# A fused two-block transformer kernel: first projections on an accumulator's bank, pieces and waits moved, and the compression's first layer on four column groups

## The chip, the cores and the metric

The kernel runs on one core of one Trainium2 chip. The metric is the device time of one execution in microseconds, the median of three runs. The kernel is one program in which TensorE (matmul), VectorE, ScalarE, GpSimd and SyncE (which issues the DMAs) each run their own list of instructions and wait for one another on semaphores.

## The reference

The input is one sequence of 256 tokens with 1024 features. Two layers with adaptive norms come first. Each takes six vectors of scales, shifts and gates from a conditioning vector, `silu(c) @ ada_w + ada_b`. Layer 0 mixes with a state-space part and latent attention, layer 1 with gated linear attention (GLA) and a sparse attention (NSA); each is followed by a SwiGLU network of width 2816. A second block follows with windowed attention and a gated MLP side by side, cross attention over 256 memory rows, and a lookup among 16384 experts (PEER). What the change touches, cut down:

```python
h = rmsnorm(x, pre) * (1.0 + scale) + shift          # ahead of every stage
gq, gk, gv, glr, gg, nq, nkv, ngate = split(h @ w_in)  # layer 1's projections
log_a = log_sigmoid(glr @ w_gk2 + b_gk) / 16
swiglu = (silu(h @ w_gate) * (h @ w_up)) @ w_down

def compress(z, w1, w2):                             # NSA, for keys and for values
    zb = z[:, win_idx] + cmp_pos                     # 15 windows of 32 tokens, 2 groups
    zb = zb.reshape(b, 15, 2, 32 * 64)               # 30 rows of 2048
    return silu(zb @ w1) @ w2                        # w1 is 2048 x 256
```

All products keep fp32 precision.

## The kernel before

**Weights.** A weight matrix comes in slabs of 128 x 2048 fp32 through a ring of three slots (`raw`). Each slab is two blocks of 1024 columns. For a block, ScalarE writes the rounded high part `whi` (`cut_hi`, L2583) and then VectorE or GpSimd the remainder `wlo` (`cut_lo`, L1487; which of the two `lo_engine` says: VectorE for the projections, by turns for the feed-forward slabs, GpSimd for the second block of the slabs in `FIRST` and for most of the peer stage). The ring of `whi`/`wlo` has three blocks, so a block's high part waits until TensorE has used the block three before it (`emptied`). A product takes three matmuls: high x high, high x low of the activations, low x high (`pe_mm3`, L601 to L603). SyncE sends the slabs in one fixed order, each when the slab three before it has been cut.

**Ada pieces.** The conditioning weights come as 0.5 MB pieces (`ADA`), two at a time in `ada_ring`. VectorE multiplies each into an accumulator (`ve_ada`, L1513, L1516). After each fourth piece TensorE sums it over partitions (`pe_ada`, L807, 8 matmul records), and VectorE adds the bias (L1505). Where the calls stand in the two engines' lists decides when the work is done. `pe_ada` also notes before which slab SyncE is to issue the next piece (`W.due() - sooner`), and SyncE then waits until the piece two before it has been used.

**Banks.** PSUM has eight banks. `Banks.take` gives the next one of the current order (`ALL` all eight, `ROT` banks 4 to 7, `ACC` the accumulators 0 to 3) and makes TensorE wait until the bank's last holder was read.

**A norm and the first projection.** At a junction the row norms are made by ScalarE and VectorE, `pe_norm` transposes the eight feature tiles into four banks (L740), with a few matmuls of no use to keep TensorE at work (L734, L723). ScalarE then writes the high part of each tile (`se_normed`, L2712 or L2710), VectorE the low part (`ve_normed`, L1599 or L1582) and only with that the banks are marked as read. The first projection (`pe_first`) goes tile by tile: high parts (L657, and L659 with the first half's low weights) for tiles 0 to 3, then the products with the low parts of h (L663) for 0 to 3, the same for 4 to 7, and last the second half's low weights (L670). This happens ahead of `ffn0` (about 237 us), `mix1` (440), `ffn1` (688), `mix2` (883) and the peer stage (1131).

**mix1.** Slabs w_gqk 0, w_glr 0, w_gqk 1 to 3. After w_gqk 1 TensorE computes `log_a` (L1080), VectorE copies it (L2006), ScalarE takes Abs, Exp, Ln, and VectorE the log gate and a scan (L2011 to L2018).

**mix2.** `ve_mix2` waits for the tables cos2 and sin2, which are sent once `ffn1` has ended, before it cuts the blocks of w_mqk.

**The compression.** `ve_windows` (L2123) gathers the 30 windows into `zb`, 16 tiles of 128 x 30. `pe_cmp_hidden` (L1181) multiplies them with 16 tiles of the raw fp32 slab, 128 x 256 each, and sums into 30 partitions. ScalarE applies Silu (L2990), `pe_cmp_turn` transposes (L1190), VectorE copies (L2130). Kind 0 is the keys, kind 1 the values. Between the two stand the GLA states (L1156 on TensorE, L2084 and L2086 on VectorE), the projection w_nq 1 and several ada pieces; the GLA outputs (L1139, L1142) follow. Then come w_nks and w_nvs and, at 607.71 us, the first use of the compression's results (L1247). An fp32 matmul leaves two records in the trace.

Of the kernel before, what the change touches and what calls it, by code (L numbers as in the profile page):

```python
# [39 lines left out]
      ("inv", 1), ("sgn", 1), ("j16", 16), ("ind", 8), ("pick", 16)]  # L40
# [275 lines left out]
class Memory:  # L316
# [90 lines left out]
    def second_layer(self):  # L407
# [18 lines left out]
        self.w2, self.zb, self.hid = alloc(256, 4, 64), alloc(480, 16, 30), alloc(256)[0:30, :]  # L426
# [125 lines left out]
class Net:  # L552
# [70 lines left out]
    def pe_linear(self, e, name, i, kt, nn, xh, xl, split=None, eager=False, ada=True):  # L623


        if ada:
            self.pe_ada(e)
        ps = self.banks.take(e, name, i)
        if split:
            self.pe_first(e, name, i, kt, [[ps[:, j * 256:(j + 1) * 256]] * 2 for j in range(nn)], [0], xh, xl, split,  # L630
                          [("full", name, i) if j == nn - 1 else None for j in range(nn)])
            if eager:
                self.pe_ada(e)
            return
# [8 lines left out]
    def pe_first(self, e, name, i, kt, outs, starts, xh, xl, split, full):  # L643


        nn = len(outs)
        for k0 in range(0, kt, 4):
            for k in range(k0, k0 + 4):
                e.wait_ge(*self.at("hi", split, k))
                for j in range(nn):  # L650
# [7 lines left out]
                    if j == 0:  # L658
                        e.matmul(outs[0][0], lo, xh[:, k, :], start=False, stop=False, skip_group_check=True)  # L659
            for k in range(k0, k0 + 4):  # L660
                e.wait_ge(*self.at("lo", split, k))
                for j in range(nn):
                    t = e.matmul(outs[j][1], self.W.high(name, (i * nn + j) * kt + k)[1], xl[:, k, :], start=False,  # L663
                                 stop=j == 0 and k == kt - 1, skip_group_check=True)
                    if j == 0 and k == kt - 1:
                        t.then_inc(*self.P(("used", self.W.high(name, i * nn * kt + k)[0]), *([full[0]] if full[0] else [])))
        for j in range(1, nn):
            for k in range(kt):
                _, lo, end = self.W.tile(e, name, (i * nn + j) * kt + k)
                t = e.matmul(outs[j][0], lo, xh[:, k, :], start=False, stop=k == kt - 1, skip_group_check=True)  # L670
            t.then_inc(*self.P(("used", end), *([full[j]] if full[j] else [])))

    def pe_linear_halves(self, e, name, i, split=None):


        self.pe_ada(e)
        if split:
            banks = [self.banks.take(e, name, i, j) for j in range(2)]
            self.pe_first(e, name, i, 8, [[ps[:, 0:T], ps[:, T:2 * T]] for ps in banks], [0, 1], self.m.hH, self.m.hL, split,
                          [("full", name, i, j) for j in range(2)])  # L680
            return
        for n in range(16):
# [345 lines left out]
    def pe_ffn(self, e, layer):  # L1028
        m = self.m
        self.P.mark("end", f"mixer{layer}", "P")  # L1030
        self.pe_norm(e, f"ffn{layer}")
        for i in range(11):
            if layer:
                self.pe_linear_halves(e, "w_gate1", i, None if i else "ffn1")
                self.pe_linear_halves(e, "w_up1", i)
            else:
                self.pe_linear(e, "w_gate0", i, 8, 2, m.hH, m.hL, None if i else "ffn0")
                self.pe_linear(e, "w_up0", i, 8, 2, m.hH, m.hL)
# [26 lines left out]
    def pe_mix1(self, e):  # L1065
# [3 lines left out]
        self.banks.order = ALL  # L1069
# [14 lines left out]
    def pe_gla(self, e):  # L1084
# [41 lines left out]
        self.pe_pieces(e, 1)  # L1126
        self.pe_cmp_hidden(e, 1)
        self.pe_pieces(e, 3, 2)
        self.pe_cmp_turn(e, 1)
        e.wait_ge(*self.at("out", "gla_state", 2, 2))  # L1130
        for h in range(4):
            if h == 3:
                self.pe_pieces(e, 1, 2)
# [11 lines left out]
            t.then_inc(*self.P(("full", "gla_o", h)))  # L1145
        self.P.mark("end", "gla", "P")
# [27 lines left out]
    def pe_cmp_hidden(self, e, kind):  # L1174
        m = self.m
        e.wait_ge(*self.at("windows", kind))
        ps = self.banks.take(e, "cmp_hidden", kind)
        for i in range(2):
            w = self.W.whole(e, "cmp_w1", 2 * kind + i).rearrange("p (k c) -> p k c", k=8)
            for k in range(8):  # L1180
                t = e.matmul(ps[0:30, 0:256], m.zb[:, 8 * i + k, :], w[:, k, :], start=i == 0 and k == 0,  # L1181
                             stop=i == 1 and k == 7, skip_group_check=True)
            t.then_inc(*self.P(("whole", "cmp_w1", 2 * kind + i), *([("full", "cmp_hidden", kind)] if i else [])))

    def pe_cmp_turn(self, e, kind):
# [3 lines left out]
        for ht in range(2):  # L1189
            t = e.transpose(ps[:, ht * 30:ht * 30 + 30], m.hid[:, ht * 128:(ht + 1) * 128], m.kc("ident", 0, 30, 30))  # L1190
# [44 lines left out]
    def pe_nsa(self, e):  # L1235
# [5 lines left out]
        self.pe_linear_tok(e, "w_nvs", 0, 8, m.hH, m.hL, ada=False)  # L1241
        e.wait_ge(*self.at("hvx"))
# [40 lines left out]
    def pe_mix2(self, e):  # L1283
# [3 lines left out]
        self.banks.order = ALL  # L1287
# [91 lines left out]
    def pe_route(self, e):  # L1379
        m = self.m  # L1380
        self.pe_norm(e, "peer")
        self.banks.order = ALL
# [2222 lines left out]
```

## Time and profile before

| | |
|---|---|
| time, median of 3 runs | 1973.27 us (1973.13 to 1975.18) |
| profiled execution, its own time | 1975.42 us |
| its span in the profile | 1973.3 us |
| TensorE matmul busy | 1880.8 us, 95% |
| VectorE busy | 1440.1 us, 73% |
| ScalarE busy | 990.5 us, 50% |
| GpSimd busy | 257.5 us, 13% |

The page divides the span into 40 slices; TensorE is at 80 to 100% in nearly all of them. In a timeline a line gives the start, the length of the merged instructions and, in brackets, the idle time before them and who ended it.

### The profile page before, as it was taken

What the parts mean: (1) busy time and instruction counts of PE and PEld (TensorE: products, weight loads), DVE (VectorE), ACT (ScalarE), POOL (GpSimd) and SP (SyncE); (2) the same over time, 40 slices, a digit from 0 to 9 for tenths busy, and PEclk for the clock granted to TensorE, in tenths of its full rate; (3) what the DMA queues carried; (4) which work ended last, traced back from release to release, by engine and by line L of the source; (5) the groups of instructions that cost most, each with busy time, mean ns of one, the idle gap of its engine ahead of it and who ended that gap; (6) DMA issues with size and microseconds to landing.
All of it is one profiled execution on the core that took longest, in us unless ns stands there. A gap on an engine that the chain in (4) does not pass through costs nothing.

```text
span 1973.3 us, 31794 instructions
## 1 busy us (share of the span) xinstructions
PE 1880.8 (95%) x12456; PEld 1698.1 (86%) x12456; DVE 1440.1 (73%) x2604; ACT 990.5 (50%) x1426; POOL 257.5 (13%) x118
## 2 busy tenths in 40 slices
PE   6899899998999899998999899999999999999998
PEld 6887799988968788888898799999988888888887
DVE  5898766667757785556666559888878887777776
ACT  5555544464435544454555546566643334444444
POOL 0001044420001044430000175000000000000000
PEclk9999999999999999999999999999999999999999
DMA  8664477755554355545444244577766866455452
GB/s 316 243 205 150 140 277 247 260 187 206 181 208 178 118 208 190 183 156 207 150 150 171 107 171 171 183 217 218 216 205 256 303 237 226 180 230 197 171 207 113
DMA packets 94548, 391.87 MB, mean 199 GB/s; under 512 B 7680, under 2 KB 41776, under 8 KB 56000
## 3 DMA queue, kind: packets, MB, share of 16 engines
q1 hardware_dynamic: 94112, 389.58, 55.5%
q8 instruction: 100, 1.64, 0.3%
q14 instruction: 48, 0.39, 0.1%
q10 hardware_dynamic: 288, 0.26, 0.0%
HBM read 371.72 MB, written 15.73 MB: 196 GB/s over the span
## 4 chain that ended last, share of the span: by engine, by line
PE 77%; DVE 13%; ACT 2%; issue 2%; DMA 0%; POOL 0%; DVEq 0%; SPq 0%; ACTq 0%
PE acc L597 9%; PE ps L613 9%; PE acc L599 9%; PE acc L598 9%; PE ps L601 5%; PE ps L602 5%; PE ps L603 5%; PE ps L614 5%; PE acc L601 3%; PE acc L603 3%; PE acc L602 3%; DVE wlo L1487 2%; PE ps L1442 1%; PE acc L1442 1%; DVE arena L1516 1%
## 5 line engine op out<-in xcount | busy, mean ns | idle before, releaser
L2583 ACT ACTIVATE whi<-raw 128x1024 fp32r<-128x1024 f32 x553 | 584.1, 1059 | 447.8 <-PE acc L599 203.9
L1487 DVE TENSOR_TENSOR wlo<-raw,whi 128x1024 fp32r<-128x1024 f32 x457 | 556.1, 1223 | 293.6 <-ACT whi L2583 287.3
L1487 POOL TENSOR_TENSOR wlo<-raw,whi 128x1024 fp32r<-128x1024 f32 x96 | 240.0, 2502 | 617.2 <-ACT whi L2583 616.9
L597 PE MATMUL acc<-whi,chi 128*128 128x512 f32 x744 | 294.3, 396 | 4.3 <-DVE wlo L1487 1.9
L599 PE MATMUL acc<-wlo,chi 128*128 128x512 f32 x744 | 291.6, 392 | 0.0
L598 PE MATMUL acc<-whi,clo 128*128 128x512 f32 x744 | 291.2, 391 | 0.0
L601 PE MATMUL ps<-hpair,whi 128*128 128x256 f32 x968 | 278.3, 287 | 3.2 <-DVE wlo L1487 3.1
L613 PE MATMUL ps<-hpair,whi 128*128 128x512 f32 x784 | 278.7, 397 | 0.0
L602 PE MATMUL ps<-hpair,whi 128*128 128x256 f32 x968 | 274.0, 283 | 0.0
L603 PE MATMUL ps<-hpair,wlo 128*128 128x256 f32 x968 | 274.0, 283 | 0.0
L614 PE MATMUL ps<-hpair,wlo 128*128 128x256 f32 x784 | 219.8, 280 | 0.0
L601 PE MATMUL acc<-hpair,whi 128*128 128x256 f32 x656 | 190.3, 290 | 9.8 <-DVE wlo L1487 9.1
L601 PEld LDWEIGHTS ps<-hpair,whi 128*128 128x128 f32 x968 | 185.9, 192 | 5.4 <-issue 3.3
L603 PE MATMUL acc<-hpair,wlo 128*128 128x256 f32 x656 | 186.4, 284 | 0.0
L602 PE MATMUL acc<-hpair,whi 128*128 128x256 f32 x656 | 186.4, 284 | 0.0
L602 PEld LDWEIGHTS ps<-hpair,whi 128*128 128x128 f32 x968 | 185.9, 192 | 0.3
L603 PEld LDWEIGHTS ps<-hpair,wlo 128*128 128x128 f32 x968 | 185.8, 192 | 0.0
L613 PEld LDWEIGHTS ps<-hpair,whi 128*128 128x128 f32 x784 | 147.3, 188 | 35.3
L597 PEld LDWEIGHTS acc<-whi,chi 128*128 128x128 f32 x744 | 140.2, 188 | 36.4 <-issue 2.9
L599 PEld LDWEIGHTS acc<-wlo,chi 128*128 128x128 f32 x744 | 140.4, 189 | 31.4
L598 PEld LDWEIGHTS acc<-whi,clo 128*128 128x128 f32 x744 | 140.5, 189 | 27.1
L614 PEld LDWEIGHTS ps<-hpair,wlo 128*128 128x128 f32 x784 | 147.9, 189 | 2.5
(513 smaller groups left out, 3087.5 us busy)
## 6 DMA issues: line engine op xcount, KB each, us to landing
raw<-in_peer_down SPq DMA_DIRECT2D x64, 1024.0 KB, 4.9
raw<-in_peer_up SPq DMA_DIRECT2D x64, 1024.0 KB, 5.0
arena<-in_ada SPq DMA_DIRECT2D x80, 512.0 KB, 4.7
raw<-in_w_gate SPq DMA_DIRECT2D x22, 1024.0 KB, 4.8
raw<-in_w_up SPq DMA_DIRECT2D x22, 1024.0 KB, 5.1
raw<-in_w_down SPq DMA_DIRECT2D x22, 1024.0 KB, 4.8
arena<-spill SPq DMA_DIRECT2D x14, 1024.0 KB, 6.9
spill<-hT_t SPq DMA_DIRECT2D x22, 448.0 KB, 6.1
```

The costliest lines, as they stand in the source:

```text
L597: e.matmul(out, xh, hi, start=start, stop=False, skip_group_check=True)
L598: e.matmul(out, xl, hi, start=False, stop=False, skip_group_check=True)
L599: i = e.matmul(out, xh, lo, start=False, stop=stop, skip_group_check=True)
L601: e.matmul(out, hi, xh, start=start, stop=False, skip_group_check=True)
L602: e.matmul(out, hi, xl, start=False, stop=False, skip_group_check=True)
L603: i = e.matmul(out, lo, xh, start=False, stop=stop, skip_group_check=True)
L613: e.matmul(ps.rearrange("p (s t) -> p s t", s=2), hi, self.m.hP[:, k], start=k == 0, stop=False, skip_group_check=True)
L614: i = e.matmul(ps[:, 0:T], lo, self.m.hH[:, k, :], start=False, stop=k == 7, skip_group_check=True)
L1442: t = e.matmul(ps[:, i * 128:(i + 1) * 128], m.oh1[:, n % 3, i * 128:(i + 1) * 128], m.oh2[n % 3][:, i * 128:(i + 1) * 128], start=True, s ...
L1487: e.tensor_tensor(out=lo, in0=w, in1=hi.bitcast(F32), op=ALU.subtract).then_inc(*X(("lo", j)))
L1516: e.scalar_tensor_tensor(out=m.ada_acc, in0=w, scalar=c, in1=m.ada_acc, op0=ALU.mult, op1=ALU.add).then_inc(*V(*([("ada", s)] if k else [])))
L2583: e.activation(hi, w, ACT.Copy, scale=1.0).then_inc(*self.A(("hi", j)))
```

## The change

It makes these edits. (1) The first projection of `ffn0` and `ffn1` takes a bank of the accumulators (`order = ACC`, back to `ROT` behind it); `mix1`, `mix2` and the peer stage restart the turn of the banks at 0, which is an accumulator. (2) In `pe_linear` and `pe_linear_halves` with a split, `pe_ada` comes behind the projection. (3) In `pe_first`, where the second block's low part is GpSimd's, the second half's low weights go ahead of the last four tiles' low products. (4) VectorE cuts the next block's low part ahead of the ada piece at the first projection (`first=True`). (5) The ada piece of w_gqk 2 moves to VectorE's list right behind the copies of `log_a`. (6) The waits for cos2 and sin2 move to the first rope. (7) `pe_cmp_hidden` takes 32 columns of `zb` at a time and writes tile k to the partitions 32*(k % 4), so that four partial sums stand in four column groups; ScalarE copies them, `pe_cmp_turn` multiplies with a 0/1 matrix `groups` that adds the four and transposes, and ScalarE applies Silu to the result; VectorE's copy is gone. (8) VectorE makes kind 1's windows ahead of the states; the turns and ada pieces near the end of `gla` move.

```diff
@@ pe_linear
-        if ada:
+        if ada and not split:
             self.pe_ada(e)
         ps = self.banks.take(e, name, i)
         if split:
             self.pe_first(...)
+            if ada:
+                self.pe_ada(e, 1)
@@ pe_first
+        early = nn > 1 and self.W.lo_engine(self.W.high(name, (i * nn + 1) * kt)[0]) == "G"
+        def second_lows():
+            for j in range(1, nn):
+                for k in range(kt):
+                    _, lo, end = self.W.tile(e, name, (i * nn + j) * kt + k)
+                    t = e.matmul(outs[j][0], lo, xh[:, k, :], start=False, stop=not early and k == kt - 1, ...)
         for k0 in range(0, kt, 4):
...
+            if early and k0 + 4 == kt:
+                second_lows()
             for k in range(k0, k0 + 4):
                 e.wait_ge(*self.at("lo", split, k))
...
+        if not early:
+            second_lows()
@@ pe_ffn
+            if i == 0:
+                self.banks.order = ACC
                 self.pe_linear(e, "w_gate0", i, 8, 2, m.hH, m.hL, None if i else "ffn0")
+                self.banks.order = ROT
@@ pe_mix1, pe_mix2, pe_route
-        self.banks.order = ALL
+        self.banks.order, self.banks.turn = ALL, 0
@@ pe_gla
         self.pe_linear(e, "w_nq", 1, 8, 2, m.hH, m.hL)
-        self.pe_pieces(e, 1)
         self.pe_cmp_hidden(e, 1)
-        self.pe_pieces(e, 3, 2)
-        self.pe_cmp_turn(e, 1)
+        self.pe_pieces(e, 1, 2)
         e.wait_ge(*self.at("out", "gla_state", 2, 2))
         for h in range(4):
-            if h == 3:
-                self.pe_pieces(e, 1, 2)
+            if h == 1:
+                self.pe_cmp_turn(e, 1)
+                self.pe_pieces(e, 2, 2)
...
+        self.pe_pieces(e, 2, 2)
@@ pe_cmp_hidden
-                t = e.matmul(ps[0:30, 0:256], m.zb[:, 8 * i + k, :], w[:, k, :], start=i == 0 and k == 0, ...)
+                n, r = 8 * i + k, 32 * (k % 4)
+                t = e.matmul(ps[r:r + 32, 0:256], m.zb32[n], w[:, k, :], start=n < 4, stop=n >= 12, ...)
@@ pe_cmp_turn
-            t = e.transpose(ps[:, ht * 30:ht * 30 + 30], m.hid[:, ht * 128:(ht + 1) * 128], m.kc("ident", 0, 30, 30))
+            t = e.matmul(ps[:, ht * 30:ht * 30 + 30], m.hid[:, ht * 128:(ht + 1) * 128], m.kc("groups"), ...)
@@ ve_linear
+        if first:
+            self.cut_lo(e, self.V, self.W.last(name, nn * kt - 1) + 1)
@@ ve_mix1
-            self.ve_linear(e, "w_gqk", i, 8, 2)
+            self.ve_linear(e, "w_gqk", i, 8, 2, ada=i != 2, first=i == 0)
... (i == 1, behind the copies of log_a)
+                self.ve_ada(e)
                 self.ve_cuts(e, "w_gqk", 47)
@@ ve_gla
         self.ve_pieces(e, 3)
+        self.ve_windows(e, 1)
         (states)
-            if c == 0:
-                self.ve_cmp_turn(e, 0)
         self.ve_linear(e, "w_nq", 1, 8, 2)
-        self.ve_windows(e, 1)
-        self.ve_pieces(e, 4)
-        self.ve_cmp_turn(e, 1)
-        self.ve_pieces(e, 1)
+        self.ve_pieces(e, 2)
+        self.ve_pieces(e, 3)
@@ ve_mix2 -> ve_rope, part 0
-        for name in ("cos2", "sin2"):
-            e.wait_ge(self.landed[name], 16)
+            for name in ("cos2", "sin2"):
+                e.wait_ge(self.landed[name], 16)
@@ se_cmp_hidden, se_cmp_turn (new, called behind gg's Silu and behind gla_o 0)
-        e.activation(m.hid, self.banks.tile("cmp_hidden", kind)[0:30, 0:256], ACT.Silu, scale=1.0)
+        e.activation(m.hid, self.banks.tile("cmp_hidden", kind)[:, 0:256], ACT.Copy, scale=1.0)
+        e.activation((m.hk, m.hv)[kind][:, :, 0:15], self.banks.tile("cmp_turn", kind)[:, 0:60]..., ACT.Silu, scale=1.0)
```

## Rows read from the trace of the kernel before

**Rows 1.** The page: busy time of the engines, share of the span, instructions
```profile
PE 1880.8 (95%) x12456; PEld 1698.1 (86%) x12456; DVE 1440.1 (73%) x2604; ACT 990.5 (50%) x1426; POOL 257.5 (13%) x118
```
**Rows 2.** Timeline of PE: start, length, line, [idle before <- who ended it]
```profile
236.82 0.39 PE L657 MATMUL ps<-hpair,whi 128*128 128x256 f32 x1 [1.91 <-DVE hpair L1599]
439.18 1.13 PE L807 MATMUL ps<-kc_t,arena 128*128 128x128 f32 x8 [2.00 <-DVE hpair L1599]
469.08 2.08 PE L807 MATMUL ps<-kc_t,arena 128*128 128x128 f32 x8 [6.52 <-DVE arena L1516]
552.88 8.78 PE L1181 MATMUL ps<-raw,arena 128*30 128x256 f32 x32 [2.33 <-DVE arena L2123]
575.27 7.09 PE L1181 MATMUL acc<-raw,arena 128*30 128x256 f32 x32 [2.50 <-DVE arena L2123]
687.71 0.55 PE L657 MATMUL ps<-hpair,whi 128*128 128x256 f32 x1 [2.56 <-DVE hpair L1599]
894.08 0.55 PE L601 MATMUL acc<-hpair,whi 128*128 128x256 f32 x1 [4.89 <-DVE wlo L1487]
1131.63 0.38 PE L657 MATMUL ps<-hpair,whi 128*128 128x256 f32 x1 [1.19 <-DVE hpair L1582]
```
**Rows 3.** Windows: busy PE, PEld, DVE, ACT, POOL, then granted clock, DMA, GB/s
```profile
467.50:471.90 4.40, 2.82 (x13) 2.82 (x14) 2.16 (x5) 0.00 (x0) 0.00 (x0) 0.50 0.44 147
893.00:898.60 5.60, 4.52 (x21) 4.55 (x22) 3.20 (x3) 0.00 (x0) 0.00 (x0) 0.50 0.90 340
687.00:690.30 3.30, 2.60 (x12) 2.63 (x13) 2.75 (x6) 2.94 (x6) 0.00 (x0) 0.53 0.86 295
554.20:557.20 3.00, 3.00 (x8) 1.23 (x7) 0.27 (x1) 0.00 (x0) 0.00 (x0) 0.50 0.98 352
575.30:582.30 7.00, 7.00 (x33) 3.35 (x33) 1.50 (x2) 0.00 (x0) 0.00 (x0) 1.00 0.72 256
```
**Rows 4.** Timelines at ffn0: ACT, PE, POOL
```profile
238.38 1.02 ACT L2712 ACTIVATE hpair<-ps,mod_t,gs_t 128x256 fp32r<-128x256 f32 x2 [0.36 <-DVE hT_t L1592]
241.72 1.12 PE L670 MATMUL ps<-hpair,wlo 128*128 128x256 f32 x8
243.02 2.40 POOL L1487 TENSOR_TENSOR wlo<-raw,whi 128x1024 fp32r<-128x1024 f32 x1 [7.00 <-ACT whi L2583]
```
**Rows 5.** Timelines in mix1: ACT, DVE, SP
```profile
440.64 1.02 ACT L2712 ACTIVATE hpair<-ps,mod_t,gs_t 128x256 fp32r<-128x256 f32 x2 [0.37 <-DVE hT_t L1592]
456.65 0.88 DVE L2006 TENSOR_SCALAR arena<-ps,pv_t 128x256 f32<-128x256 f32 x2
460.69 2.36 DVE L1487 TENSOR_TENSOR wlo<-raw,whi 128x1024 fp32r<-128x1024 f32 x2 [3.16 <-ACT whi L2583]
449.09 0.33 SPq L3373 DMA_DIRECT2D arena<-in_ada  x1
```
**Rows 6.** Timelines at ffn1: POOL, PE
```profile
690.65 2.85 POOL L1487 TENSOR_TENSOR wlo<-raw,whi 128x1024 fp32r<-128x1024 f32 x1 [4.38 <-ACT whi L2583]
694.82 0.40 PE L613 MATMUL ps<-hpair,whi 128*128 128x512 f32 x1
```
**Rows 7.** Timeline of POOL at the peer stage
```profile
1137.82 7.09 POOL L1487 TENSOR_TENSOR wlo<-raw,whi 128x1024 fp32r<-128x1024 f32 x3 [1.53 <-ACT whi L2583]
```
**Rows 8.** Timelines at mix2: ACT, DVE
```profile
885.50 1.11 ACT L2583 ACTIVATE whi<-raw 128x1024 fp32r<-128x1024 f32 x1
892.71 3.50 DVE L1487 TENSOR_TENSOR wlo<-raw,whi 128x1024 fp32r<-128x1024 f32 x3 [5.97 <-DMA arena<-in_sin]
```
**Rows 9.** Groups of PE by shape: count, busy us, mean ns, idle before
```profile
L980 PE MATMUL acc<-arena,raw 128*64 128x256 f32 x32 | 7.1, 380 | 0.8 <-ACT arena L2838 0.8
L862 PE MATMUL acc<-arena 128*64 128x128 f32 x32 | 2.0, 275 | 1.1 <-DVE arena L1721 1.1
```
**Rows 10.** Timelines in the compression: SP, DVE
```profile
551.09 13.40 SPq L3373 DMA_DIRECT2D arena<-in_ada  x3
598.95 1.23 DVE L1487 TENSOR_TENSOR wlo<-raw,whi 128x1024 fp32r<-128x1024 f32 x1 [5.67 <-ACT whi L2583]
```

## Prediction of the change's time

> **What bounds the kernel now.** I read the page's shares first [rows 1]: TensorE is busy for 95% of the span, and no other engine for more than 73%. So a gain can only be idle time of TensorE, work of TensorE that is taken out, or a stretch at its lower clock. Next I took TensorE's timeline, listed its waits, and went by the edits of the diff to those that they touch. There are eight [rows 2]: 1.91, 2.00, 6.52, 2.33, 2.50, 2.56, 4.89 and 1.19 us, 23.9 us in all. Then the windows around them [rows 3]: behind the waits of 6.52, 4.89, 2.56 and 2.33 us the granted clock is about 0.50 for 3 to 5.6 us, which is 1.2 of 2.4 GHz; behind the 2.50 it stayed at 1.00. These four stretches hold 16 us. Between waits TensorE issues matmuls at a fixed distance: 8 of 128x256 take 1.12 us with 0.28 for the last one [rows 4], so 0.12 each; at the lower clock 21 of them take 4.52, so 0.215 each [rows 3]. One slab of a projection, 48 of them, is 5.76 us, and one block of 1024 weight columns, 24 of them, 2.88 us.
>
> **Part 1, first projection after a norm (five junctions).** `pe_first` waited for the bank of the norm's transposes, that is for VectorE's low part of h (releasers L1599 and L1582 in [rows 2]). In the change it takes an accumulator's bank, read before the norm began, and can start at the first high part. But its end is set by the last high part: 3 matmuls, the 8 of the second half's low weights, now put ahead, and the 8 with the low part of h come behind it. At ffn0: ScalarE's last pair ends at 239.4, 239.4 + 19 x 0.12 = 241.7, against 241.72 + 1.12 = 242.8 before [rows 4]. That is 1.1 us. Next is late block 3 of the weights. Its high part needs block 0 free, at 241.7 in both orders, then GpSimd takes 2.40 and has it ready at 245.4 [rows 4]. TensorE would want it at 241.75 + 2.88 = 244.6 and waits 0.8; it came at 245.9 before. **0.5 us** is left.
> At mix1 all low weights but one are VectorE's at 1.2 us a block, so that limit is absent; the reduction of an ada piece (8 records, 0.9 us) goes from ahead of the projection to behind it. Before, TensorE ran without a break from 439.18 [rows 2]: 0.9 + 5.8, until 445.9. In the change: last high part 441.66 [rows 5], 19 matmuls 2.28, reduction 0.95, 444.9: **1.0 us**.
> At ffn1 block 2 is GpSimd's. It runs from 690.65 to 693.50 behind ScalarE's high part and nothing in the change moves it; TensorE began that block at 694.82 [rows 6]. It would be through with the first slab at 691.95 and waits until 693.5: **1.3 us**, the lower clock of this stretch being covered by the wait.
> At the peer stage TensorE starts 1.1 us sooner, but the next blocks are GpSimd's again, three in a row from 1137.82 [rows 7], and start only 0.2 sooner, by the same freeing as at ffn0: **0.4 us**. At mix2 no row shows a wait for the bank: 0.
> VectorE's part (`first=True`: the next block's low weights ahead of the ada piece) is the same instructions in another order; it has block 2 ready at 241.6 at ffn0. Queued behind it is the ada piece, later by one block's 1.22 us, for which only the next reduction waits, two slabs on. On SP `pe_ada` keeps its place: it is called one slab further on, and `sooner=1` takes that back.
>
> **Part 2, the ada piece of mix1.** TensorE stood 6.52 us at 469.08 for a piece that VectorE did behind its chain of log gates and scans [rows 2]. Moved, it runs behind L2006, which ends at 457.5 (456.5 with part 1's gain), for 1.54 us. Its data was issued by SP at 449.09, so it has landed. Queued behind it on VectorE are the two low weights that started at 460.69 and waited 3.16 us for ScalarE [rows 5]: they lose nothing, nor does TensorE, which wants them at 462. So the whole wait goes, and with it the lower clock behind it: the reduction took 1.7 us in place of 0.9 and six matmuls 0.21 in place of 0.12. 6.5 + 1.4 = **7.9 us**. What is late next: VectorE is 3 us less ahead of TensorE in the levels of GLA, where no wait of TensorE shows; I cost it at nothing, and at 1 us if that cover is thin.
>
> **Part 3, cos2 and sin2.** VectorE stood 5.97 us for sin2 before it cut mqk 1's low weights [rows 8]; TensorE stood 4.89 for those and then worked at 0.50 until 898.6 [rows 2, 3]. Behind the edit the wait stands at the first rope, in step i=2 of `ve_mix2`, after 899, when the tables are there. ScalarE's high part ended at 886.6, and VectorE was free at 892.71 - 5.97 = 886.7 [rows 8]: low part at 888.0, TensorE there at 889.1, no wait. 4.9, and 21 matmuls at 0.21 in place of 0.12, which is 2.0: **6.9 us**.
>
> **Part 4, the compression.** Each kind is 16 fp32 matmuls of 30 columns (32 records), 7.09 us for the second and 8.78 for the first, of which 3.0 at the lower clock [rows 2, 3]. The change runs them on four groups of 32 columns. No row has four groups. The nearest: the attention heads (L862), 16 matmuls with 128 moving columns on two column groups, 2.0 us for 32 records; L980 has 64 columns on one group and takes 7.1 us for 32 records with 256 moving columns, so 3.55 for 128 [rows 9]. Two groups come close to half the time. I take four at a quarter: 6.8/4 + 0.3 = 2.0 us; bounds 2.0 and 7.1 (one after another), 3.7 if two run at once.
> The Trainium skill, "TensorE: Matmul & The Clock Gate", Part 3 on packing small matmuls, measures 2.38 times for three column tiles; no run here shows it. Carried to four that would be some 3.2 times, an estimate: 2.2 us a kind and 0.4 us less gain in all.
> First kind: start 552.9 as before (one more memset of 4 columns, at most 0.1), end 555.0. The reduction behind it (1.2) now falls into the lower clock and ends at 557.0; before, 562.7: **5.6 us**. Second kind: windows 1 come ahead of the states on VectorE, so the 2.50 wait goes, and 7.1 becomes 2.0: **7.5 us**. What is late next, worked out by the same steps: windows 1 stand at 561.2 on VectorE and are needed at 567; its states end at 565.9, needed at 569.0. The ada piece whose reduction now stands at head 1 ends at 571.4, needed at 571.5. SP can send the second kind's slabs once VectorE has done the piece behind the reduction, at 558.4, where the three ada issues ended at 564.5 before [rows 10]; they land near 566, needed at 567. So two places have no slack. ScalarE's Silu behind the turn has until the first use at 594 (607.7 before). VectorE ends its pieces 9 us sooner, TensorE its part 13; VectorE stood idle 5.67 before 598.95 [rows 10], which covers that.
>
> **Sum.** 0.5 + 1.0 + 1.3 + 0.4 + 7.9 + 6.9 + 13.1 = 31.1 us. The profiled execution took 1975.42 (span 1973.3), 2.1 over the median of 1973.27; taken off its own time that is 1944.3, off the median **1942.2**.
>
> **Rivals.** (a) In fp32 the four groups run one after another: 5.1 and 5.0 us are lost, 1942.2 + 10.1 = 1952.3. For it: no row shows four; against: [rows 9] at two. (b) The compression comes to be bound by the queue. SP serves ada pieces and slabs in one order, five pieces now stand before w_out1a where four did, and if both places without slack fail by 2 us, 1946.2. (c) Slower: TensorE's clock. The packed matmuls are short and the waits at the junctions are spread in small pieces; if the clock then falls to 1.2 GHz and stays, a stretch loses 0.44 us per us (1 - 0.12/0.215). It decides from 71 us of it, when the 31.1 are eaten, and 90 us give 1982. For it: all four low stretches of [rows 3] stand at edited places. Against: each is behind a wait of 2.3 us or more, of which the change leaves one. (d) The bank is not what holds the junctions, and part 1's 3.2 are missing: 1945.4.
> The same page of the Trainium skill, Part 1, has thin work between waits put TensorE back to its cold clock each time. By that rule (c) would be likelier; the trace agrees behind the waits of 2.33, 2.56, 4.89 and 6.52 us and not behind that of 2.50 [rows 2, 3].
>
> **Chances.** Forecast with its small neighbours 0.70, (a) 0.10, (b) 0.11, (d) 0.06, (c) 0.03. The range goes from 1936.5 (the first kind's lower clock gone too, 1.5, the waits for blocks in part 1 absent, 2.7, and the skew of the runs) to 1953 and holds (a), (b) and (d). A measurement tells about 0.2%, 4 us, from no change: faster 0.96, within 0.2% 0.01, slower 0.03.
>
> **What would show it.** L657 right behind the norm's matmuls and L670's group ahead of the last L663; no wait at the reduction in mix1; no wait for sin2 ahead of mqk 1; L1181's 32 records in 2 us; granted clock 1.00 at gqk 3 and mqk 1. It would be wrong with 7 us for those records, a new wait at the reduction of head 1, or waits for GpSimd's blocks longer than 0.8 and 1.5 us.

## The result, and the profile after

The changed kernel takes **1942.3 us** (median of 4 executions, 1939.1 to 1945.3). The kernel before, run beside it, takes 1973.2 us (1969.9 to 1975.2). The ratio is 0.9848, with a 95% interval from 0.9828 to 0.9869. In the profiled execution the span fell from 1973.3 to 1941.1 us.

The page of the changed kernel begins as follows; the line answers to [rows 1]. TensorE is busy for 13.5 us less; 12 of them are the compression's records, which now share their time on four column groups.

```profile
span 1941.1 us, 31807 instructions
...
PE 1867.3 (96%) x12460; PEld 1688.7 (87%) x12460; DVE 1442.8 (74%) x2603; ACT 991.3 (51%) x1428; POOL 257.8 (13%) x118
```

**Where the time went.** A norm's first transpose stands in both traces (L740 before, L757 after), so the run can be cut at them. The table is worked out from the starts of these rows; its last row ends with TensorE's last record. The stretch from mix1 to the next norm is cut once more, at the first record of the compression (L1181, after: L1205).

| stretch | before, us | after, us | difference | forecast |
|---|---|---|---|---|
| ahead of ffn0's norm | 232.06 | 231.88 | -0.18 | 0 |
| ffn0 to mix1 | 202.27 | 202.93 | **+0.66** | -0.5 |
| mix1 to the compression | 118.56 | 109.65 | -8.91 | -8.9 |
| compression to ffn1 | 129.41 | 116.36 | -13.05 | -13.1 |
| ffn1 to mix2 | 198.55 | 197.42 | -1.13 | -1.3 |
| mix2 to the next norm | 165.74 | 158.54 | -7.20 | -6.9 |
| from there to the peer stage | 82.78 | 81.17 | **-1.61** | 0 |
| peer stage, to the end | 836.25 | 835.55 | -0.70 | -0.4 |

These lengths repeat well: in the second profile of the changed kernel (experiment 10) six of the eight are the same within 0.15 us. The other two are not: ahead of ffn0's norm it has 229.25 us, and from the compression to ffn1 118.10. Ahead of ffn0, where no edit has a part, the twelve profiles with the change or most of it go from 227.3 to 231.9 us.

**The edited places.** The timeline of TensorE in the changed kernel, at the places of [rows 2], with the idle time before a row in brackets:

```profile
245.47 0.38 PE L603 MATMUL ps<-hpair,whi 128*128 128x256 f32 x1 [0.69 <-POOL wlo L1512]
249.02 1.16 PE L824 MATMUL ps<-kc_t,arena 128*128 128x128 f32 x8 [0.42 <-DVE arena L1541]
...
444.57 1.06 PE L824 MATMUL acc<-kc_t,arena 128*128 128x128 f32 x8
461.99 1.05 PE L824 MATMUL ps<-kc_t,arena 128*128 128x128 f32 x8
...
544.46 1.93 PE L1205 MATMUL ps<-raw,arena 128*32 128x256 f32 x32 [2.35 <-DVE arena L2150]
557.76 1.07 PE L1205 MATMUL acc<-raw,arena 128*32 128x256 f32 x16
559.92 1.07 PE L1205 MATMUL acc<-raw,arena 128*32 128x256 f32 x16 [1.09 <-DMA raw<-in_cmp_w]
...
672.14 0.47 PE L615 MATMUL ps<-hpair,whi 128*128 128x512 f32 x1 [1.40 <-POOL wlo L1512]
...
1108.56 0.38 PE L603 MATMUL acc<-hpair,whi 128*128 128x256 f32 x1 [0.43 <-POOL wlo L1512]
```

The waits of 1.91, 2.00, 6.52, 2.50, 2.56, 4.89 and 1.19 us of [rows 2] are gone. Only the 2.33 ahead of the compression's first kind is left. In their place stand short waits for GpSimd's blocks (0.69, 1.40, 0.43), one for the second kind's slab (1.09) and one for an ada piece (0.42). The 32 records of a kind take 1.93 us where they took 8.78 and 7.09.

### The profile page after: what moved, and what is told of

Read it like the earlier page. It is cut to its first block, busy times and chain, and to the rows that moved or that the text cites. A ratio compares the mean times of both kernels' runs of the same rounds, so it can differ in the third digit from the quotient of the medians.

```text
span 1941.1 us, 31807 instructions
## 1 busy us (share of the span) xinstructions
PE 1867.3 (96%) x12460; PEld 1688.7 (87%) x12460; DVE 1442.8 (74%) x2603; ACT 991.3 (51%) x1428; POOL 257.8 (13%) x118
## 4 chain that ended last, share of the span: by engine, by line
PE 75%; DVE 14%; ACT 2%; issue 2%; DMA 1%; POOL 0%; DVEq 0%; ACTq 0%
PE ps L615 9%; PE acc L599 9%; PE acc L601 9%; PE acc L600 9%; PE ps L616 5%; PE ps L603 5%; PE ps L604 5%; PE ps L605 5%; PE acc L603 3%; PE acc L604 3%; PE acc L605 3%; DVE wlo L1512 2%; DVE arena L1541 2%; PE acc L1467 1%; PE ps L1467 1%
## 5 line engine op out<-in xcount | busy, mean ns | idle before, releaser
L601 PE MATMUL acc<-wlo,chi 128*128 128x512 f32 x744 | 291.2, 391 | 0.0
L603 PE MATMUL ps<-hpair,whi 128*128 128x256 f32 x912 | 262.8, 288 | 4.3 <-DVE wlo L1512 3.1
L604 PE MATMUL ps<-hpair,whi 128*128 128x256 f32 x912 | 258.6, 284 | 0.0
L605 PE MATMUL ps<-hpair,wlo 128*128 128x256 f32 x912 | 258.5, 283 | 0.0
L616 PE MATMUL ps<-hpair,wlo 128*128 128x256 f32 x784 | 219.8, 280 | 0.0
L603 PE MATMUL acc<-hpair,whi 128*128 128x256 f32 x712 | 205.3, 288 | 4.3 <-DVE wlo L1512 3.6
L604 PE MATMUL acc<-hpair,whi 128*128 128x256 f32 x712 | 201.3, 283 | 0.0
L605 PE MATMUL acc<-hpair,wlo 128*128 128x256 f32 x712 | 201.3, 283 | 0.0
L603 PEld LDWEIGHTS ps<-hpair,whi 128*128 128x128 f32 x912 | 175.4, 192 | 6.4 <-issue 2.6
L615 PEld LDWEIGHTS ps<-hpair,whi 128*128 128x128 f32 x784 | 147.3, 188 | 36.9 <-issue 1.6
L604 PEld LDWEIGHTS ps<-hpair,whi 128*128 128x128 f32 x912 | 175.5, 192 | 0.3
L605 PEld LDWEIGHTS ps<-hpair,wlo 128*128 128x128 f32 x912 | 175.3, 192 | 0.0
L601 PEld LDWEIGHTS acc<-wlo,chi 128*128 128x128 f32 x744 | 139.9, 188 | 31.6
L616 PEld LDWEIGHTS ps<-hpair,wlo 128*128 128x128 f32 x784 | 147.9, 189 | 2.5
```

Source lines behind the costliest of these rows:

```text
L601: i = e.matmul(out, xh, lo, start=False, stop=stop, skip_group_check=True)
L603: e.matmul(out, hi, xh, start=start, stop=False, skip_group_check=True)
L604: e.matmul(out, hi, xl, start=False, stop=False, skip_group_check=True)
L605: i = e.matmul(out, lo, xh, start=False, stop=stop, skip_group_check=True)
L615: e.matmul(ps.rearrange("p (s t) -> p s t", s=2), hi, self.m.hP[:, k], start=k == 0, stop=False, skip_group_check=True)
L616: i = e.matmul(ps[:, 0:T], lo, self.m.hH[:, k, :], start=False, stop=k == 7, skip_group_check=True)
```

## The experiments

Each is the changed kernel with one edit; only the ninth adds to the eighth, and the last is a combination.

**1. The packing: the same matmuls, group after group.**

```diff
-                n, r = 8 * i + k, 32 * (k % 4)
-                t = e.matmul(ps[r:r + 32, 0:256], ..., start=n < 4, stop=n >= 12, ...)
+                n, r = 8 * i + k, 32 * ((8 * i + k) // 4)
+                t = e.matmul(ps[r:r + 32, 0:256], ..., start=n % 4 == 0, stop=n % 4 == 3, ...)
```

> The 16 products of a kind keep their shape and their four groups of partitions, but stand in the order 0,0,0,0,1,1,1,1,..., so that neighbours are on the same group and can't run beside one another. Theory (what pays is that matmuls on different column groups run at the same time): 32 records take 7.1 us again in place of 1.93, in each kind. Kind 0 costs 5.2; kind 1 costs 5.2 less the wait of 1.09 for its second slab, which is then covered, so 4.1. In all +9.3 us, 1951.6, and up to 3 more if the lower clock of the kernel before comes back in kind 0. Rival (the gain comes from the other shape, 32 columns and windows 30 columns apart, and from the moved Silu and windows): 32 records stay near 2 us and the time at 1942.3.

Measured: 1945.05 us (1942.8 to 1952.1; ratio to before 0.9861, 0.9837 to 0.9885). The timeline of TensorE in this kernel:

```profile
541.64 6.08 PE L1205 MATMUL ps<-raw,arena 128*32 128x256 f32 x32 [2.35 <-DVE arena L2150]
559.08 4.60 PE L1205 MATMUL acc<-raw,arena 128*32 128x256 f32 x32
```

Both expectations missed: the time rose by 2.7 us where 9.3 or nothing was expected, and 4.60 us lies between 7.1 and 1.93. The first kind lies in a stretch of lower clock here (0.50 of full speed from 542 to 544), so the second is the one to read. The starts of its single records show why. Within a group a record begins 0.216 us after the one before. But group 1 begins 0.89 us after group 0, together with the fifth of group 0's eight records, and so on: 3 x 0.893 + 8 x 0.216 + 0.19 = 4.6. So the records do not start in the order of the program: the first one of group 2, which waits for the second slab, starts at 560.87 us, and the last one of group 1, which reports the first slab as used, only at 561.51. "Serial" was not serial, then, and the experiment tells the price of the order rather than that of the packing.

**2. Two groups at a time.**

```diff
-                n, r = 8 * i + k, 32 * (k % 4)
-                t = e.matmul(ps[r:r + 32, 0:256], ..., start=n < 4, stop=n >= 12, ...)
+                n, r = 8 * i + k, 32 * (k % 2 + 2 * i)
+                t = e.matmul(ps[r:r + 32, 0:256], ..., start=k < 2, stop=k >= 6, ...)
```

> The same products on two groups at a time (first slab on groups 0 and 1, second on 2 and 3). Theory of overlap by group: half the speed of four, 3.6 to 3.9 us a kind; kind 0 +1.8, kind 1 +1.8 less the covered wait of 1.09, so +2.5 us, 1944.8. Rival (two groups are as good as four, the rest is bound by the moving columns): 1.93 us, 0.

Measured: 1942.71 us (1941.4 to 1944.6; 0.9844, 0.9828 to 0.9860), which can't be told from the changed kernel; the trace tells more.

```profile
539.87 2.82 PE L1205 MATMUL ps<-raw,arena 128*32 128x256 f32 x32 [2.35 <-DVE arena L2150]
554.11 1.92 PE L1205 MATMUL acc<-raw,arena 128*32 128x256 f32 x16
556.60 1.92 PE L1205 MATMUL acc<-raw,arena 128*32 128x256 f32 x16 [0.57 <-DMA raw<-in_cmp_w]
```

Not 3.6 to 3.9 us but 2.82 (the first kind), by the same overlap: 0.893 + 8 x 0.216 + 0.19 = 2.81. Each half alone takes 1.92 for 16 records on two groups, where four groups take 1.07.

**3. Thirteen of the sixteen on one group.** This run tests that arithmetic, written down before it ran.

```diff
-                n, r = 8 * i + k, 32 * (k % 4)
-                t = e.matmul(ps[r:r + 32, 0:256], ..., start=n < 4, stop=n >= 12, ...)
+                n = 8 * i + k
+                r = 32 * n if n < 4 else 0
+                t = e.matmul(ps[r:r + 32, 0:256], ..., start=n < 4, stop=0 < n < 4 or n == 15, ...)
```

> The first four products of a kind go to the four groups, the other twelve to group 0, which so has 13 of them, 26 records. In the run of four serial groups a record followed the one before it on the same group after 0.216 us, and the next group's first one began once the group before had started half of its eight records. Theory (a record holds its own group for 0.216 us, and only the longest group sets the time, with issue running some four records ahead): 26 x 0.216 + 0.2 = 5.8 us a kind; kind 0 +3.9, kind 1 +2.8 (the wait of 1.09 for its slab is covered), 1949.0. Rival (any use of all four groups, or the mere shape of 32 columns, is what pays): 2 to 4.6 us a kind as in the runs before.

Measured: 1949.41 us (1946.2 to 1949.9; 0.9871, 0.9846 to 0.9895), against 1949.0.

```profile
542.29 7.17 PE L1206 MATMUL ps<-raw,arena 128*32 128x256 f32 x32 [2.36 <-DVE arena L2151]
560.82 5.88 PE L1206 MATMUL acc<-raw,arena 128*32 128x256 f32 x32
```

5.88 us against 5.8; the first kind has 1.4 us more, again from the lower clock. The rival, that the mere shape pays, is out. The same sum gives the kernel before: 32 x 0.216 + 0.2 = 7.1, where [rows 2] has 7.09. With the groups taken by turns, the time of a kind is thus the chain of its longest group: 8 records in the changed kernel, 32 in the kernel before. Issued group after group, 8 records a group took 4.60 us all the same (experiment 1).

The Trainium skill, "TensorE: Matmul & The Clock Gate", Part 3 on packing small matmuls, has 2.38 times for three column tiles. These runs show four: 7.09 to 1.93 us, 3.7 times, so the forecast's 2.0 held and the 2.2 us carried over from that page was a little too long.

**4. The ada piece of mix1 back in its place.**

```diff
-            self.ve_linear(e, "w_gqk", i, 8, 2, ada=i != 2, first=i == 0)
+            self.ve_linear(e, "w_gqk", i, 8, 2, first=i == 0)
...
-                self.ve_ada(e)
                 self.ve_cuts(e, "w_gqk", 47)
```

> The ada piece of w_gqk 2 goes back to its place behind the log gates and scans. Theory (part 2 of the sum): the wait of 6.5 us at the reduction comes back and with it 1.4 us of lower clock, +7.9 us, 1950.2. Rival 1 (the gain of mix1 came mainly from the junction): less than 4. Rival 2 (the lower clock has another cause): +6.5 with the granted clock at 1.00 behind the wait.

Measured: 1951.20 us (1950.2 to 1953.2; 0.9888, 0.9871 to 0.9904), +8.9 on the changed kernel. The timeline, and the windows with the granted clock in the third column from the right:

```profile
464.93 1.44 PE L824 MATMUL ps<-kc_t,arena 128*128 128x128 f32 x5 [6.52 <-DVE arena L1541]
```
```profile
463.00:466.00 3.00, 1.07 (x5) 1.07 (x6) 1.74 (x3) 0.00 (x0) 0.00 (x0) 0.50 0.10 12
466.00:470.00 4.00, 4.00 (x20) 4.00 (x20) 2.44 (x4) 0.00 (x0) 0.00 (x0) 0.50 0.96 384
470.00:470.50 0.50, 0.50 (x4) 0.50 (x4) 0.00 (x0) 0.00 (x0) 0.00 (x0) 0.50 0.97 393
```

The wait is back to the hundredth, and so is the lower clock. The stretch from mix1 to the compression takes 118.80 us: 9.15 more, of which 6.5 wait and 2.6 clock. Against the kernel before (118.56) it is 0.2 longer, though its junction is the new one. The junction's gain is not lost at the wait: the reduction starts 33.86 us behind the norm's first transpose (464.93 - 431.07), and 34.76 before (469.08 - 434.32). It is lost behind it. In the profile of this kernel the lower clock lasts until 5.6 us behind that start, while in the kernel before the full clock is back 3.1 us behind it:

```profile
472.20:475.50 3.30, 3.30 (x30) 3.30 (x29) 1.48 (x2) 0.87 (x1) 0.00 (x0) 1.00 0.97 397
```

With 0.44 us lost per us at the lower clock, these 2.5 us come to 1.1 us, an estimate.

**5. The waits for cos2 and sin2 back.**

```diff
+        for name in ("cos2", "sin2"):
+            e.wait_ge(self.landed[name], 16)
         for i in range(4):
             self.ve_linear(e, "w_mqk", i, 8, 2)
```

> The waits for cos2 and sin2 stand ahead of the first slab of mix2 again. Theory (part 3): 4.9 us of wait and 2.0 of lower clock come back, +6.9 us, 1949.2; the tables are sent some 22 us earlier together with everything else, so the wait keeps its size. Rival (the junction's new order moves the wait or covers it): under 5.

Measured: 1949.53 us (1947.4 to 1951.7; 0.9880, 0.9863 to 0.9896), +7.2.

```profile
869.15 0.45 PE L603 MATMUL acc<-hpair,whi 128*128 128x256 f32 x1 [4.48 <-DVE wlo L1512]
```
```profile
869.00:873.00 4.00, 3.85 (x20) 3.88 (x21) 2.27 (x3) 0.00 (x0) 0.00 (x0) 0.57 0.92 325
```

The profile has 6.20 us more in this stretch (164.74): 4.48 of wait and, with a shorter stretch at the lower clock than in [rows 3], 1.7 behind it. The part was priced rightly.

**6. The banks back.**

```diff
-            if i == 0:
-                self.banks.order = ACC
...
-        self.banks.order, self.banks.turn = ALL, 0
+        self.banks.order = ALL
```

> The banks of the first projections are taken as in the kernel before, so that the projection waits again for VectorE's low part; the new order inside it, the other moves and the compression stay. Theory (the bank holds the junctions): mix1 +1.0, ffn1 +1.3 less what the new order inside keeps, peer +0.4, ffn0 between 0 and +0.7, in all +2 to +3 us, 1944.3 to 1945.3, with waits of 1 to 2.6 us on VectorE at the first projections. Rival (d) (the bank isn't what holds them): no change, 1942.3.

Measured: 1946.49 us (1945.1 to 1948.1; 0.9862, 0.9839 to 0.9884), +4.2. By stretches: ffn0 -0.14, mix1 +2.33, ffn1 +0.59, mix2 0, peer +1.29. The timeline at ffn1 and the peer stage, and a window of mix1:

```profile
666.44 0.35 PE L673 MATMUL ps<-hpair,whi 128*128 128x256 f32 x1 [2.56 <-DVE hpair L1622]
...
1102.62 0.39 PE L673 MATMUL ps<-hpair,whi 128*128 128x256 f32 x1 [1.18 <-DVE hpair L1605]
```
```profile
436.00:440.00 4.00, 4.00 (x23) 4.00 (x23) 3.09 (x5) 2.52 (x5) 0.00 (x0) 0.57 0.63 250
```

The waits of 2.56 and 1.19 us on VectorE are there again, and so are those at ffn0 and mix1 (1.91 us each), so it was the bank that held the junctions: rival (d) is out. The new order inside the projection and the later reduction stayed in this kernel; no run takes those two back. At ffn1 only 0.59 of the 2.56 are a loss, since the later TensorE finds GpSimd's block ready and is spared the 1.40. Of the 2.33 in mix1 the lower clock takes some 1.5, an estimate from the 4 us at a mean of 0.57. That leaves 0.8 against the 1.0 forecast, and accounts for most of what came beyond the +2 to +3 expected. At ffn0 the bank brings nothing.

**7. VectorE's order at ffn0.**

```diff
-                self.ve_linear(e, "w_gate0", i, 8, 2, first=i == 0)
+                self.ve_linear(e, "w_gate0", i, 8, 2)
```

> Only the ada piece of w_gate0 0 goes back ahead of the next block's low weights on VectorE; the rest is as in the changed kernel. There VectorE's four steps of two pieces took 7.34 us from 241.63, of which 5.70 beside GpSimd's block, and the reduction waited 0.42 us. Theory (what ate ffn0's gain is that the piece now lies beside GpSimd's blocks, where a step takes up to 3 us in place of 0.77): the first piece takes 1.54 us alone again, both are done by 246.8, no wait at the reduction; but block 2 is ready only at 243.1, so TensorE waits 1.3 there in place of 0.69 at block 3: reduction at 248.9 in place of 249.02, the time as before within 0.3 us. Rival (order on VectorE is all that counts, no contention): the steps stay as slow and the reduction comes 0.5 us later.

Measured: 1941.65 us (1940.0 to 1944.4; 0.9835, 0.9813 to 0.9857), not to be told from the changed kernel by the time. The trace decides. First the changed kernel, VectorE and GpSimd:

```profile
241.63 7.34 DVE L1541 SCALAR_TENSOR_TENSOR arena<-arena,gs_t 128x512 f32<-128x512 f32 x4
243.27 5.70 DVE L1541 SCALAR_TENSOR_TENSOR arena<-arena,gs_t 128x512 f32<-128x512 f32 x2
```
```profile
242.95 2.47 POOL L1512 TENSOR_TENSOR wlo<-raw,whi 128x1024 fp32r<-128x1024 f32 x1 [7.07 <-ACT whi L2603]
246.02 2.40 POOL L1512 TENSOR_TENSOR wlo<-raw,whi 128x1024 fp32r<-128x1024 f32 x1 [0.60 <-ACT whi L2603]
```

The second row is the view from 243.2 on: the last two of the four steps, 5.70 us. Then the experiment, VectorE, GpSimd and TensorE:

```profile
239.20 1.54 DVE L1541 SCALAR_TENSOR_TENSOR arena<-arena,gs_t 128x512 f32<-128x512 f32 x2
240.66 1.22 DVE L1512 TENSOR_TENSOR wlo<-raw,whi 128x1024 fp32r<-128x1024 f32 x1
241.98 3.56 DVE L1541 SCALAR_TENSOR_TENSOR arena<-arena,gs_t 128x512 f32<-128x512 f32 x2
```
```profile
242.07 2.92 POOL L1512 TENSOR_TENSOR wlo<-raw,whi 128x1024 fp32r<-128x1024 f32 x1 [7.07 <-ACT whi L2603]
```
```profile
242.03 0.35 PE L603 MATMUL ps<-hpair,whi 128*128 128x256 f32 x1 [1.10 <-DVE wlo L1512]
```

Alone two steps take 1.54 us, so 0.77 each. Beside a block of GpSimd one of them takes about as long as the block: the one of 243.27 ends at 245.96, GpSimd's at 245.42; the next at 248.97, GpSimd's at 248.42. Started late, two steps met two blocks and took 5.70; in the experiment they met one and took 3.56. The waits of the changed kernel (0.69, 0.42, and 0.3 more behind the reduction, for the block that VectorE began only at 248.89) become one of 1.10, and ffn0 takes 202.40 us in place of 202.93. The reduction comes 0.12 sooner, as expected; the other 0.4 are the wait behind it, which the expectation had overlooked.

The Trainium skill, "SBUF — State Buffer", "Who interferes with whom", says that a VectorE instruction with two inputs in SBUF contends with a GpSimd instruction that reads there, and calls the port pair that the two share an exclusive lock. The trace agrees: a step of 0.77 us, begun beside a block of 2.4 us, ended only 0.55 us behind the block's end.

**8. The late slab.** The wait of 1.09 us is for kind 1's second slab. The third ada piece is issued behind the slabs:

```diff
         self.pe_cmp_hidden(e, 0)
-        self.pe_pieces(e, 3, 2)
+        self.pe_pieces(e, 2, 2)
+        self.pe_pieces(e, 1)
```

> The third ada piece behind kind 0 is issued behind kind 1's slabs. Theory (kind 1's wait of 1.09 us is for a slab that stands on SP's queue behind three ada pieces): the slab lands 2 to 2.5 us sooner and the wait goes, but the piece that comes later moves all the following, and the reduction ahead of head 1 waits 1.5 to 2 us: net +0.5 to +1 us or no change. Rival (the slab is late by its own transfer, not by its place): the wait of 1.09 stays.

Measured: 1942.81 us (1942.3 to 1947.4; 0.9851, 0.9827 to 0.9876).

```profile
554.15 1.93 PE L1206 MATMUL acc<-raw,arena 128*32 128x256 f32 x32
560.11 1.16 PE L824 MATMUL ps<-kc_t,arena 128*128 128x128 f32 x8 [1.22 <-DVE arena L1542]
```

As expected: the wait for the slab is gone, and the reduction waits 1.22 us for the piece instead. Rival (b) named the right place and the right engine; the price was 1.1 us, not 4.

**9. The reduction later as well.**

```diff
-            if h == 1:
                 self.pe_cmp_turn(e, 1)
+            if h == 3:
                 self.pe_pieces(e, 2, 2)
```

> As the run before, and the reduction that stood ahead of head 1 goes ahead of head 3, some 4.5 us later. Theory: neither the slab nor the piece is waited for, -1.1 us, 1941.2. Rival (the reduction's later place makes w_nks or the first use of the compression wait): 0 or a loss.

Measured: 1945.54 us (1942.5 to 1947.5; 0.9861, 0.9838 to 0.9884). From the first kind to the end of gla it takes 25.49 us in place of 26.79, the 1.3 that were wanted. But the next stretch, nsa, grows from 89.6 to 93.4. TensorE comes 1.3 us sooner and VectorE does not: its first block behind gla begins 34.7 us behind the first kind's start, against 33.9 in the changed kernel. So TensorE waits 1.21 us at 577.15 for that block, and nearly all that was won is gone. VectorE stood 3.44 us for the later reduction, but also 1.73 and 1.07 us for the data of its pieces; no run tells which of them made it late. The other 2.6 us are not shown to be the edit's. The first scores waited 1.47 us where the changed kernel has 0.76, but in experiment 7, with gla as in the changed kernel, they waited 1.48; and a second stretch at the lower clock (0.50 from 624.6 to 628) costs some 1.5, an estimate. The timelines of VectorE and TensorE, then TensorE's at the first scores in experiment 7:

```profile
564.54 0.16 DVE L1532 TENSOR_TENSOR mod_t<-ps,pv_t 128x4 f32<-128x4 f32 x1 [3.44 <-PE ps L824]
```
```profile
577.15 0.36 PE L599 MATMUL ps<-whi,hpair 128*128 128x256 f32 x1 [1.21 <-DVE wlo L1514]
```
```profile
588.92 1.75 PE L1232 MATMUL ps<-arena 64*128 64x128 f32 x16 [1.48 <-DVE arena L2188]
```

The rival held: its place was w_nks or the compression's first use, and the wait of 1.21 us stands between the two.

**10. A combination, beside the changed kernel once more.** The combination takes the edits 7, 8 and 9 and moves VectorE's last piece of gla, with TensorE's call for its reduction, to the end of nsa (VectorE's side is shown):

```diff
-        self.ve_pieces(e, 3)
+        self.ve_pieces(e, 2)
...
+        self.ve_ada(e)
         self.ve_bank_split(e, "nsa1", m.hH, m.hL, 1)
```

> The changed kernel with four moves: the ada piece of w_gate0 0 ahead of the next block again; the third ada piece behind kind 1's slabs; the reduction ahead of head 3; and VectorE's last ada piece of gla moved to the middle of its idle time ahead of the last split of nsa, since with the first three alone VectorE came 1.21 us late for the first block behind gla and 1.48 late at the first scores. Theory: ffn0 -0.54, gla -1.3, the wait of 0.77 at the first scores gone, in all -2.6 us, 1939.7 if the changed kernel is at 1942.3. Rival (the moved piece makes the last stretch of nsa late): what is won at 589 is lost again at 640 to 660, -0.5 or none.

> The changed kernel once more, beside the one before. Theory: median 1942.3 within 2 us, the edited places (waits of 0.69, 0.42, 1.09, 1.40 us; 32 records in 1.93) the same within 0.1. [...]

Measured: the combination 1940.46 us (5 executions, 1938.0 to 1943.4; 0.9830, 0.9808 to 0.9851), the changed kernel 1942.52 (5 executions, 1940.5 to 1945.1; 0.9843, 0.9822 to 0.9865). The intervals overlap widely, so the 2.1 us are not shown. In the profiles ffn0 has its 0.5 and gla 1.0, but nsa takes 91.1 us against 90.0. The rival expected a loss in nsa, but at 640 to 660 us. Here the first scores waited 0.25 us and the next turn 3.27, which no run takes apart; the kernel before has these same two waits, so the moved piece need not be their cause. The row of the combination, and that of the kernel before:

```profile
596.94 1.94 PE L865 MATMUL ps<-kc_t,arena 128*128 128x128 f32 x8 [3.27 <-DVE arena L1743]
```
```profile
620.53 1.06 PE L848 MATMUL ps<-kc_t,arena 128*128 128x128 f32 x8 [3.27 <-DVE arena L1713]
```

The second profile of the changed kernel shows what differs from one execution to the next. Its first kind, and the window around it:

```profile
541.83 3.37 PE L1205 MATMUL ps<-raw,arena 128*32 128x256 f32 x32 [2.35 <-DVE arena L2150]
```
```profile
541.00:545.00 4.00, 3.17 (x32) 1.39 (x32) 2.27 (x4) 0.35 (x1) 0.00 (x0) 0.57 0.87 356
```

Here the lower clock did follow the wait of 2.35, and the same records took 3.37 us. In the first profile it did not: 1.93 us, granted clock 1.00 from 544 to 548. Of the twelve profiles five have the lower clock at the first kind (experiments 1, 3, 6 and both of this one) and seven have not.

## Why the prediction was right, and where it was not

The forecast was 1942.2 us, the time is 1942.3. The sum of 31.1 us stands against 32.2 in the two spans and 30.9 between the medians. That it comes so near is in part luck. In the table the six stretches with edits give 30.3 us, 0.8 less than their sum; the other 1.8 stand where no edit is. And what the clock does in a single execution moves a profile by more than the 0.1 us between forecast and median: the compression's stretch differs by 1.7 us between the two profiles of the changed kernel. Its terms, in its own order:

**Part 1** was to bring 3.2 us and brought 2.0. *ffn0* is the step that failed: -0.5 forecast, +0.66 measured. The junction itself gave 1.2 us (the first row behind it, L603, stands 9.79 behind the norm's first transpose; L601 stood 11.01 behind it), and GpSimd's block came where it was put (0.69 us of wait against 0.8). But from start to start the three waits cost 0.85, 0.58 and 0.31 us. The failed sentence is that of `first=True`: "the same instructions in another order", with the ada piece later by 1.22 us and nobody but a reduction two slabs on waiting for it. A later piece fell beside GpSimd's blocks and took 5.70 us in place of 3.73, and both the reduction and the next block came late. The trace of before could have warned. These are its steps alone, and beside GpSimd's block of [rows 4]:

```profile
240.25 1.54 DVE L1516 SCALAR_TENSOR_TENSOR arena<-arena,gs_t 128x512 f32<-128x512 f32 x2
243.03 3.73 DVE L1516 SCALAR_TENSOR_TENSOR arena<-arena,gs_t 128x512 f32<-128x512 f32 x2
```

Putting the pieces back (experiment 7) brings 0.5 of it. The rest is a trade: there TensorE waits 1.10 for VectorE's block, which then stands behind the piece.

*mix1*: TensorE's run through the junction ended at 444.57 + 1.06, which is 10.8 us behind the norm's first transpose; before it was 11.6 (445.9 - 434.3), so 0.8 of the 1.0. *ffn1*: 1.13 of 1.3, the wait for GpSimd's block 1.40 against 1.5. *Peer*: 0.70 where 0.4 was forecast, and 1.3 against the kernel with the banks back (experiment 6). *mix2*: 0, as forecast.

**Part 2**, 7.9 us: with the junction the stretch gave 8.91 against 8.9; less the junction's 0.8 that is 8.1. Experiment 4 gives 9.15 for the removal alone: the same wait of 6.52 us, and 2.6 of lower clock where the forecast had 1.4. In that one profile the lower clock lasted longer than in the kernel before.

**Part 3**, 6.9 us: 7.20 by the stretch, 6.2 by the profile of experiment 5 and 7.2 by its median.

**Part 4**, 13.1 us: 12.9 up to the end of gla. Two errors made up for each other. The records took 1.93 against 2.0. The first kind gave 6.8 and not 5.6 us, since the lower clock that the forecast put behind it did not come in this execution; in the second profile it came, and up to the end of gla 11.6 us were gained in place of 12.9. The second gave 6.1 and not 7.5, of which 1.1 for a slab that landed late: one of the two places "without slack". The other, the piece at head 1, held; the reduction there has no wait.

**An unforeseen term.** At 1107 us, at no edited place, the profile of before has a stretch at the lower clock which the one of after has not. The rows are TensorE's 32 records there and the window, of before, then the same two of after, and the records once more in the kernel of experiment 8:

```profile
1106.92 5.44 PE L1372 MATMUL ps<-arena 128*128 128x128 f32 x32 [1.42 <-DVE arena L1721]
```
```profile
1107.00:1110.00 3.00, 3.00 (x15) 3.00 (x16) 0.00 (x0) 0.00 (x0) 0.00 (x0) 0.51 0.79 328
```
```profile
1077.11 3.81 PE L1397 MATMUL ps<-arena 128*128 128x128 f32 x32 [1.42 <-DVE arena L1748]
```
```profile
1077.00:1081.00 4.00, 3.81 (x32) 3.65 (x32) 0.69 (x1) 0.64 (x2) 0.00 (x0) 1.00 0.62 250
```
```profile
1074.44 5.44 PE L1398 MATMUL ps<-arena 128*128 128x128 f32 x32 [1.42 <-DVE arena L1749]
```

The wait ahead of them is 1.42 us in all three. 3.81 or 5.44 us is the whole difference of 1.6. Among the twelve profiles of kernels with the change or most of it, this stretch is at the lower clock in two (experiments 6 and 8). So it is a matter of the single execution, and the 1.6 us are no gain of the change as far as these runs show. Whether the change makes it rarer, with one profile of before, stays open. Without it the two spans differ by 30.6, which the forecast overshot by 0.5.

**The rivals.** (a) is out by experiments 1 to 3, (d) by 6. (b) was half true and is priced at 1.1 us by 8. (c) is out; the clock went the other way: the mean granted clock was 0.986 to 0.993 in executions of before and 0.993 to 0.997 in those of after.

## What to carry to other kernels

Small matmuls on column groups cost what the longest group's chain costs; spread them evenly and take the groups by turns. Before putting off a VectorE step with two SBUF inputs, look which of GpSimd's instructions it will then lie beside. A wait that is removed is worth what the next wait on the same engine leaves of it (at ffn1 0.59 us of 2.56, experiment 6), so price the edits of one stretch together and not one by one. Where the clock follows a wait in one execution and not in the next, one profile gives its price only within that swing.

## What the runs showed of the hardware

- An fp32 matmul with 32 columns and 256 moving ones leaves two records, and each holds its column group for 0.216 us. Four groups run at once (32 records in 1.93 us). With eight records on one group and the next eight on another, the other group's first record started with the fifth of the first group's, ahead of three that stand before it in the program.
- Two SCALAR_TENSOR_TENSOR steps of 128x512 on VectorE take 1.54 us alone, 3.56 beside one block of GpSimd and 5.70 beside two. GpSimd's blocks took 2.40 and 2.47 us in the one order, 2.57 and 2.92 in the other.
- At the same place, behind the same wait, TensorE's clock fell in some executions and in others not: behind 2.35 us ahead of the first kind (1.93 or 3.37 us for the records), behind 1.42 us at 1077 (3.81 or 5.44). The spread of the executions goes with it: of the changed kernel the slowest of the five, 1945.1 us, had a mean granted clock of 0.993, and the fastest, 1940.5, had 0.997.
- The length of nsa differed by up to 4 us (89.1 to 93.4) between profiles of kernels that differ little. Of the 93.4 a wait of 1.21 us is explained here; the waits at the first scores went from 0.25 to 1.48 us without an edit near them, and why stays open.
